# Memory's keys and values as the mixer's last projection units, and the output projection by token halves

## The reference

```python
x = x + 0.5 * swiglu(rmsnorm(x, ffn1_norm), ...)
h = rmsnorm(x, mix_norm)
q, k, v, z_rwkv, gate_a, gate_b = split(h @ w_in)
merged = sigmoid(gate_a) * window_attention(q, k, v) + sigmoid(gate_b) * rwkv7(z_rwkv)
x = x + merged @ w_out
# cross attention, 4 heads of width 256 into the 256 memory tokens
hq, m = rmsnorm(x, cross_norm), rmsnorm(mem, mem_norm)
mk, mv = split(m @ w_ckv)                  # (256, 1024) each
x = x + (softmax((hq @ w_cq) @ mk.T / 16) @ mv) @ w_co
x = x + 0.5 * swiglu(rmsnorm(x, ffn2_norm), ...)
out = rmsnorm(x, final_norm)
```

## Time and profile before

| | us |
|---|---|
| median of 3 runs (3301.2 to 3301.44) | 3301.32 |
| the profiled execution | 3303.52 |
| its span | 3301.7 |
| mean granted TensorE clock, share of 2.4 GHz | 0.947 |

### The profile page before, as it was taken

How to read it: one execution, slowest core, us unless ns; L and a number is a source line. 1 busy time by engine, 2 the same in 40 slices (tenths; PEclk the granted TensorE clock), 3 DMA queues, 4 the chain that set the end, 5 groups by cost and what they waited for, 6 DMA issues and landing times. The chain is left out here.

```text
span 3301.7 us, 61575 instructions
## 1 busy us (share of the span) xinstructions
PE 2963.9 (90%) x26974; PEld 2434.4 (74%) x26974; DVE 1598.2 (48%) x1747; ACT 1055.4 (32%) x1718; POOL 1300.2 (39%) x667
## 2 busy tenths in 40 slices
PE   3899999996899999999999986797976799999995
PEld 2688888884678877787877765786755588887885
DVE  6654444444166556656655662113222744453445
ACT  2433333222234334433434432212121333333221
POOL 1344444442364545455544541222131344444441
PEclk7999999997999999999999986898988899999997
DMA  3222224433221111322111100611002222234441
GB/s 139 80 96 80 80 103 166 144 121 134 59 62 58 52 45 45 96 63 63 52 45 45 53 21 9 229 52 32 19 26 89 64 80 77 78 108 159 144 144 67
DMA packets 247432, 270.71 MB, mean 82 GB/s; under 512 B 13184, under 2 KB 204800, under 8 KB 245120
## 3 DMA queue, kind: packets, MB, share of 16 engines
q1 hardware_dynamic: 247168, 266.81, 24.6%
HBM read 218.54 MB, written 48.23 MB: 81 GB/s over the span
## 5 line engine op out<-in xcount | busy, mean ns | idle before, releaser
L459 POOL TENSOR_TENSOR w_low<-ffn_work,w_high 128x1024 fp32r<-128x1024 f32 x182 | 445.0, 2446 | 668.6 <-ACT w_high L532 393.9
L499 PE MATMUL bank<-h_high,w_high 128*128 128x512 f32 x1232 | 484.6, 393 | 57.6 <-DVE h_low L643 34.6
L499 PE MATMUL bank<-h_low,w_high 128*128 128x512 f32 x1232 | 483.3, 392 | 0.0
L499 PE MATMUL bank<-h_high,w_low 128*128 128x512 f32 x1232 | 482.9, 392 | 0.0
L1076 POOL TENSOR_TENSOR mix_panel_low<-arena,mix_panel_high 128x1024 fp32r<-128x1024 f32 x96 | 233.0, 2427 | 343.6 <-ACT mix_panel_high L1442 343.6
L1171 PE MATMUL bank<-mix_h_high,mix_panel_high 128*128 128x512 f32 x768 | 317.6, 414 | 20.0 <-POOL mix_panel_low L1076 14.9
L690 DVE TENSOR_TENSOR h_low<-ffn_work,h_high 128x512 fp32r<-128x512 f32 x88 | 205.7, 2337 | 250.7 <-ACT h_high L547 250.7
L499 PEld LDWEIGHTS bank<-h_high,w_high 128*128 128x128 f32 x1232 | 233.9, 190 | 110.9 <-issue 60.1
L1171 PE MATMUL bank<-mix_h_low,mix_panel_high 128*128 128x512 f32 x768 | 304.4, 396 | 0.0
L1171 PE MATMUL bank<-mix_h_high,mix_panel_low 128*128 128x512 f32 x768 | 303.3, 395 | 0.0
L516 PE MATMUL bank<-h_high,w_high 128*128 128x512 f32 x704 | 275.2, 391 | 4.6 <-DVE h_low L690 4.6
(11 more groups left out here) (263 smaller groups left out, 5822.8 us busy)
## 6 DMA issues: line engine op xcount, KB each, us to landing
arena<-w_in SPq DMA_DIRECT2D x96, 512.0 KB, 3.8
ffn_work<-w_down SPq DMA_DIRECT2D x88, 512.0 KB, 3.6
a_spill<-ffn_work SPq DMA_DIRECT2D x88, 256.0 KB, 2.3
ffn_work<-a_spill SPq DMA_DIRECT2D x88, 256.0 KB, 2.7
ffn_work<-w_gate SPq DMA_DIRECT2D x12, 1024.0 KB, 5.7
ffn_work<-w_up SPq DMA_DIRECT2D x12, 1024.0 KB, 8.2
arena<-x_spill SPq DMA_DIRECT2D x3, 4096.0 KB, 14.2
arena<-w_gate SPq DMA_DIRECT2D x10, 1024.0 KB, 5.6
```

The costliest lines, as they stand in the source:

```text
L459: nc.gpsimd.tensor_tensor(slot(w[1], q), src, slot(w[0], q).bitcast(F32), ALU.subtract).then_inc(s_low, 1)
L499: last = mm(bank[:, bk, :], w[wp][:, q % RING, kt, e], h[hp][:, k, kt], start=fresh and kt + wp + hp == 0, stop=kt == KT // 2 - 1 and wp = ...
```

## The change

`shared` also loads `mem`, squares, scales and transposes it (8 transposes after panel 2 and 8 after panel 3), splits it and spills both parts to HBM (`mem_spill`, 2 x 1 MB). In `mixer` the units go on past 96: 96 to 111 are the panels of `w_ckv`, multiplied in three single passes with memory's parts (24 matmuls of 256 columns), which are loaded over `h`'s first-half buffers when unit 95 is done. They take the places that `points(i)` and `inside(i)` give: five in `prepare(15)`, one in `solve(15)`, five in `prepare(16)`, four in `solve(16)`, one in `prepare(17)`. 112 and 113 are the first two panels of `w_out`, rounded and subtracted only, and 114 to 117 the merged result's first token half, read back and split into the buffers of `h`. Keys and transposed values stay in the space of the mixer's shared tensors, which now stays open through `cross`.

`cross` transposes the values (16 transposes, ScalarE copies) and multiplies `w_out` in 16 units: eight panels with the first token half, and the same eight, loaded and split again, with the second. The second half's sources are split during the first eight units. The norm is two norms of 512 tokens: the first half's sums follow unit 8, its transposes unit 9, its scaling runs during units 10 and 11; the second half's lie among the first head's query matmuls (`project_first`). The source of `w_co` is split by halves too.

```diff
+        kT, v_all, vT_mem = (kept.t[:, at:at + 2 * D].rearrange("p (a b) -> p a b", b=b)
+                             for at, b in ((0, NMEM), (2 * (CH + T), D), (2 * (CH + T) + 2 * D, NMEM)))
+        w_out, wkv = panels(d["w_out"]), panels(d["w_ckv"])
...
-                    sp.dma_start(x_spill[:, :], xT[:].rearrange("p a b -> p (a b)")).then_inc(s_spill, 16)
                     nrm.wait(sp, KT - 2)
                     nrm.wait(sp, KT - 1)
+                    for t in range(MT):
+                        sp.dma_start(mem_rows[t], d["mem"][t * P:(t + 1) * P, :]).then_inc(s_mem, 16)
+                    sp.dma_start(x_spill[:, :], xT[:].rearrange("p a b -> p (a b)")).then_inc(s_spill, 16)
                     for w in range(2):
                         sp.dma_start(h_spill[w], hB[w][:].rearrange("p a b -> p (a b)").bitcast(F32)).then_inc(
                             s_spill, 16)
-                    sp.wait_ge(s_spill, 48)
+                    sp.wait_ge(s_mlow, KT)
+                    for w in range(2):
+                        sp.dma_start(mem_spill[w], mem_parts[w][:].rearrange("p a b -> p (a b)").bitcast(F32)).then_inc(
+                            s_spill, 16)
...
+                        if 2 <= j < 4:
+                            if j == 2:
+                                pe.wait_ge(s_mscaled, MT)
+                            else:
+                                pe.wait_ge(s_mlow, KT // 2)
+                            for kt in range(4 * (j - 2), 4 * (j - 1)):
+                                for t in range(MT):
+                                    last = nc.tensor.transpose(mem_bank(kt)[:, t * P:(t + 1) * P],
+                                                               mem_rows[t][:, kt * P:(kt + 1) * P], c("ident"))
+                            last.then_inc(s_mtr, 1)
...
+            KV, OUT, SRC = UNITS, UNITS + 2 * KT, UNITS + 2 * KT + 2
+            ALL = SRC + KT // 2
+            mem_in = [hA[w][:, 0:KT // 2].rearrange("p a b -> p (a b)").rearrange("p (a b) -> p a b", b=NMEM)
+                      for w in range(2)]
+
+            def points(i):
+
+                if i <= ITER:
+                    return [NP * (i + 1) + j for j in range(NP - 1)]
+                return list(range(NP * (ITER + 1) + NP - 1 + 4, OUT))
+
+            def inside(i):
+
+                return [NP * (i + 2) - 1] if i < ITER else list(range(NP * (ITER + 2) - 1, NP * (ITER + 2) + 3))
 
...
+                        dst = raw[unit % 2][:]
+                        if unit < KV:
+                            src = w_in[:, :, col(unit):col(unit) + P]
+                        elif unit < OUT:
+                            src = wkv[:, :, (unit - KV) * P:(unit - KV + 1) * P]
+                        elif unit < SRC:
+                            src = w_out[:, :, (unit - OUT) * P:(unit - OUT + 1) * P]
+                        else:
+                            if unit == SRC:
+                                for j in range(2):
+                                    sp.wait_ge(s_mw[j], 16 * (PAIRS // 2))
+                            k = 2 * (unit - SRC)
+                            src = m_spill.rearrange("p (k t) -> p k t", t=T)[:, k:k + 2, 0:HALF]
+                            dst = raw[unit % 2].rearrange("p a b -> p (a b)").rearrange("p (a b) -> p a b", b=HALF)
...
+                    def load_mem():
+                        sp.wait_ge(S("proj_ready"), UNITS)
+                        for w in range(2):
+                            sp.dma_start(mem_in[w].rearrange("p a b -> p (a b)").bitcast(F32), mem_spill[w]).then_inc(
+                                s_memin, 16)
...
+                            if unit == KV and term == 0:
+                                pe.wait_ge(s_memin, 32)
+                            dst, src = bank[:, unit % 2, :], hA[hp][:, kt]
+                            if unit >= KV:
+                                dst, src = bank[:, unit % 2, 0:NMEM], mem_in[hp][:, kt]
+                            last = mm(dst, pw[wp][:, unit % 2, kt], src, start=term == 0, stop=term == TERMS - 1)
...
+                            elif not live and s >= FIRST_CHAIN:
+                                u, n = divmod(s - FIRST_CHAIN, 6)
+                                project(inside(i)[u], n * TERMS // 6, (n + 1) * TERMS // 6)
...
+                                    if not live and u > 0 and first == 0:
+                                        store(inside(i)[u - 1])
+                                        round_panel(inside(i)[u - 1] + 2)
...
+                        if k == KT:
+                            nx[0].pe_sums(pe)
+                        elif k == KT + 1:
+                            nx[0].pe_scale(pe)
...
+                    for k in range(2, KT + 2):
+                        subtract_low(pool, k % 2, k)
+                        if k >= 4:
+                            subtract_source(pool, 1, k - 4, k - 3)
+                    for kt in range(KT - 2, KT):
+                        subtract_source(pool, 1, kt, kt + 1)
+                    nx[0].pool_root(pool)
+                    for k in range(KT + 2, KT + 4):
+                        subtract_low(pool, k % 2, k)
+                    nx[0].pool_low(pool)
+                    for k in range(KT + 4, Q + 2):
+                        subtract_low(pool, k % 2, k)
 
...
+                    for k in range(KT + 2, Q + 2):
+                        round_high(act, k % 2, k, k // 2)
+                        if k == KT + 3:
+                            nx[0].act_high(act)
+                        if k > KT + 2:
+                            act.wait_ge(s_padd, k - 2)
+                            nx[1].square(act, k - KT - 3)
...
+                    def project_first():
+                        nx[0].wait(pe, KT - 2)
+                        nx[0].wait(pe, KT - 1)
+                        panel_ready(pe, Q)
+                        terms(0, 0, 0, KT // 2)
+                        nx[1].pe_sums(pe)
+                        terms(0, 0, KT // 2, KT)
+                        panel_ready(pe, Q + 1)
+                        terms(1, 0, 0, KT // 2)
+                        nx[1].pe_scale(pe)
+                        terms(1, 0, KT // 2, KT)
+                        for t in range(2):
+                            for kt in range(KT):
+                                if t == 0:
+                                    nx[1].wait(pe, kt)
+                                last = terms(t, 1, kt, kt + 1)
```

554 lines of the change are left out of this document (310 added, 244 removed).

## The result

The changed kernel takes 3277.11 us (median of four runs, 3271.20 to 3278.38) against 3301.26 before (3301.18 to 3301.44): the ratio is 0.9923, with a 95% interval of 0.9906 to 0.9940. It is faster, by 24 us where 49 were forecast. That is above the forecast's own range (3243 to 3265) and at the upper end of the wide one (3238 to 3276): the ratio applied to the 3301.32 us on record gives 3275.9. The profiled execution took 3278.38 us, with a span of 3276.6.

A forecast was written before the change was run, and what follows sets the result against it. TensorE, busy 90% of the span, was taken as the bound, so only its waits could give much. The mixer and `shared` pay 37 us, cross-attention saves 86: -49 on 3301.32 gives 3253 us, own range 3243 to 3265, wide 3238 to 3276.

The forecast's parts named there:

- prepare(15), +9: Mixer, preparing 15: GpSimd's returning panel subtractions slow VectorE's operations, from 28.6 to about 37.6 us.
- prepare(16), +8: Mixer, preparing 16: 11.0 us is too short for five panels; the last unit ends 18.7 us in.
- if the ring keeps up it is +2: Mixer, preparing 16: if panels are loaded, rounded and subtracted in time, the stage costs only 2 us more.
- solve(16), +4 at the full clock: Mixer, last solve: four units fit at full clock; ScalarE's stores and roundings between the chain's copies show about 4 us.
- the clock stays low: Last solve, within the dear units rival (0.21): at the low clock the stage costs +16 us instead of +4.
- prepare(17) and the end, +12: Mixer's end: the last two merged pieces load behind the last write, 26 us after the chain instead of 14.
- `w_out` stage, 100.7 us: Cross-attention: 3.7 transposes, 87.4 matmuls, 1.2 low clock, 7.5 late panels and 0.9 norm matmuls.
- hidden by 0.5 us: `w_out` stage, panel 4: lands about 24 us in behind 7 MB of loads and is used at 28.
- The two late places that I did forecast: `w_out` stage: 2.5 us late behind source pieces when unit 8 starts, and 4.9 us for panel 12 behind norm roundings.
- Norm and queries, 30.5 us: After the last `w_out` unit: the second half's norm and first head's queries end at 30.5 us, against 47.6 before.
- The slower rival: `w_out` stage: raw panels don't overlap, a unit takes 9.55 us, sixteen cost 65 more, total 3318 us; chance 0.04.
- The rival of dear units: Key and value units: low clock in solve(16) or weight loads setting the pace, +20 us, total 3273; chance 0.21.

The follow-up runs named there:

- the experiment on that wait: Changed kernel with TensorE waiting, before the last solve, for VectorE's scaling of the chunk outputs instead of the merged half: 3270.53 us, ratio 0.9907.
- the edits of panels 4, 12 and 13: Changed kernel with panel 4 loaded earlier, panels 12 and 13 handled between norm splits, last merged pieces' loads ahead of the write: 3259.89 us.

## Why the prediction was right in sign and off in size

- **prepare(15), +9:** +8.1, for the greater part by VectorE's operations under GpSimd's subtractions, as forecast: VectorE is busy for 6.5 us more, and 5.0 us go with the subtractions. TensorE waited 5.2 us for memory's parts, which were ready some 9 us after their issue and not 7; VectorE waited 0.6 us for it, so that cover held, but for little.
- **solve(15), +2:** +2.1.
- **prepare(16), +8:** +12.7. The last unit was forecast to end 18.7 us in, and ScalarE stored it 18.8 us in, but that is partly luck. The forecast had TensorE wait for GpSimd's panels; the trace has no such wait over 0.3 us, and with subtractions of 0.46 us the stage still took 18.36 us, +6.9. TensorE's units and the stage's other matmuls fill it, which "if the ring keeps up it is +2" left out. "Solving starts there" was the step that failed for the time. The slow VectorE operations, which I had priced in prepare(15), occur here too (2.84 and 2.77 us for 0.69), and the chain waits for the last of them: 4.6 us, as the experiment on that wait showed, and 2.4 or nothing in other traces.
- **solve(16), +4 at the full clock:** +6.5. I took the full clock; the stage had 0.86, since the idle time in front of the chain lowered the clock for two chunks. At 1.00 it takes 25.6 to 25.9 us, +3. The rival "the clock stays low" was right for the first 8 us of the stage.
- **prepare(17) and the end, +12:** +12.9, with the loads of the last two pieces behind the last write as forecast. It wasn't a necessary cost.
- **`w_out` stage, 100.7 us:** 111.8. Panel 4, "hidden by 0.5 us", was late by 3.7. Rounding and subtraction were in that 0.5 (24 + 3.6 against 28); the panel was ready at 29.3, 1.7 us later, and TensorE wanted it at 25.6, 2.4 us earlier. The 28 doesn't follow from the prediction's own terms: 3.7 + 1.2 + 4 x 5.46 is 26.7, by which the panel would have been 0.9 us late. The two late places that I did forecast waited 2.9 and 5.9 us (2.5 and 4.9). And each wait for a late panel was followed by a stretch at a mean clock of 0.56 to 0.66, where I had counted the low clock once, at the start, as 1.2: TensorE is busy for 99.2 us where my terms make 93.2. With the edits of panels 4, 12 and 13 the stage took 98.5.
- **Norm and queries, 30.5 us:** 34.5. The block's end came as forecast (4.6 against 3.8); the queries themselves took 29.9 at a clock of 0.94, with six short waits for the second half's split pieces (1.4 and 1.3 us).
- **Behind it, nothing:** 2.5 us, nearly all in `w_co`, for which nothing in the trace of before spoke.
- **The slower rival** (a serial ring of raw panels in the `w_out` stage) didn't occur: units that don't wait take 5.4 to 5.5 us.
- **The rival of dear units** came nearer to the time, 3273, than the forecast did, but not by its mechanism: the key and value matmuls came 0.12 us apart, where 0.114 was forecast and 0.2275 was its bound.

In short, the parts were in the right places with roughly the right prices. What failed for the time were the start of the last solve, the low clock behind each wait, and the time at which unit 4 wants its panel.

## What to carry to other kernels

A transfer is hidden only if it lands before the first engine that handles it, with the whole chain up to the consumer in between, and a cover of 0.5 us between two estimates of some 25 us is none. Where work is added under a stage, price the slowdown that it brings in every stage in which it runs, and look at what waits for the last slowed instruction. A long wait of TensorE can cost its length and then a stretch at the lower clock: the waits of 3.7 and 5.9 us were worth 5.6 and some 8 here. Removing one stall can show the next in the same queue, as unit 13 did behind unit 12. And one trace of a kernel that varies is one draw: compare a stage over all the traces that share its code before giving a difference to an edit.

## What the runs showed of the hardware

- The granted clock can make less work slower: with a quarter of the key and value matmuls the last solve ran at 0.50 for 28.09 us, with all of them at 1.00 for 25.6 to 25.9.
- A 512-column matmul in full precision took about 0.87 us at the full clock when ten stood in a row (8.75 us), a single-pass one of the split products 0.2267.
- A 128x512 VectorE operation on two SBUF inputs that began 0.1 us behind a GpSimd subtraction took 2.84 us; one that began 0.01 us ahead of it took 0.69. Which came first was settled by when a load had landed, and with it 1.5 to 7.5 us of the kernel.
- Behind the same wait of 2.4 us the granted clock of the next 4 us was 0.54, 0.68 or 1.00, in three traces of the same code.
- Two kernels with the same 288 matmuls of one form at a clock of 1.00 took 65.24 and 67.01 us.
